# S5 mixer: state sums as TensorE matmuls, and the C array loaded once and copied on ScalarE

## The reference

```python
def s5_mixer(h, lam_re, lam_im, log_dt, b_re, b_im, c_re, c_im, d_skip, w_glu, b_glu):
    dt = jnp.exp(log_dt.astype(f32))[:, None]
    mag = jnp.exp(lr * dt)
    ab_re = mag * jnp.cos(li * dt)
    ab_im = mag * jnp.sin(li * dt)
    ...
    bu_re = jnp.einsum('blgp,gnp->blgn', u_c, bb_re)
    bu_im = jnp.einsum('blgp,gnp->blgn', u_c, bb_im)
    ...   # state s_t = ab * s_(t-1) + bu_t, complex, 64 groups x 64 states
    y = jnp.einsum('blgn,gpn->blgp', st_re, cr) - jnp.einsum('blgn,gpn->blgp', st_im, ci)
    ...
    y = (y + d_skip.astype(f32) * h.astype(f32)).astype(h.dtype)
    g = jax.nn.gelu(y)
    return g * jax.nn.sigmoid(g @ w_glu + b_glu)
```

## Time and profile before

| | us |
|---|---|
| median of three runs | 1295.19 |
| lowest and highest | 1292.33, 1297.12 |
| the profiled execution | 1296.42 |
| its span from first to last instruction | 1294.6 |

### The profile page before, as it was taken

The page is one execution under the profiler, slowest core; times in us unless marked ns, Lnnn a source line. Parts: engine busy times, 40 slices in busy tenths (PEclk is TensorE's granted clock), DMA queues, the critical chain, the costliest instruction groups (busy, mean ns, idle before and its releaser), DMA issues.

```text
span 1294.6 us, 25201 instructions
## 1 busy us (share of the span) xinstructions
PE 1247.5 (96%) x10872; PEld 1167.8 (90%) x10872; DVE 856.5 (66%) x1176; ACT 605.4 (47%) x778; POOL 51.8 (4%) x67
## 2 busy tenths in 40 slices
PE   5879999999999999999999999999999999999997
PEld 4667899999966489999999999999998999999997
DVE  6899678877547777768557565447469666666443
ACT  5854544433345465544345434336334545544342
POOL 5310000100000000000000000000000000000000
PEclk8968999999999999999999999999999999999998
DMA  9946568988742928654566554454454434655452
GB/s 261 311 152 204 200 227 287 333 290 270 223 156 93 298 93 280 208 194 155 166 199 195 163 179 162 155 177 155 145 167 149 146 131 131 196 194 188 146 179 73
DMA packets 219704, 247.01 MB, mean 191 GB/s; under 512 B 5872, under 2 KB 209088, under 8 KB 219616
## 3 DMA queue, kind: packets, MB, share of 16 engines
q1 hardware_dynamic: 211616, 218.63, 52.8%
q0 software_dynamic: 7648, 26.86, 6.1%
q10 hardware_dynamic: 352, 0.23, 0.1%
HBM read 244.66 MB, written 1.05 MB: 190 GB/s over the span
## 4 chain that ended last, share of the span: by engine, by line
PE 86%; DVE 5%; ACT 3%; DMA 3%; issue 1%; SPq 1%; DVEq 0%; ACTq 0%
PE PS L1749 85%; DMA RING<-in_ada_w 2%; SPq L441 1%; ACT PARTS L592 1%; DMA RING<-in_mla_w_uq 1%; DVE ARENA L1153 1%; DVE ARENA L1322 0%; DVE X L1157 0%; DMA RING<-in_w_in 0%; DVE ARENA L1350 0%; DVE PARTS L1011 0%; PE PS L2372 0%; DVE ARENA L1346 0%; DVE WL L1033 0%; PE PS L2088 0%
## 5 line engine op out<-in xcount | busy, mean ns | idle before, releaser
L1749 PE MATMUL PS<-PARTS 128*128 128x256 f32 (+3 forms) x3608 | 840.0, 283 | 0.0
L1749 PEld LDWEIGHTS PS<-PARTS 128*128 128x128 f32 (+1 forms) x3608 | 619.4, 189 | 1.4 <-issue 0.9
L1033 DVE TENSOR_TENSOR WL<-RING,PARTS 128x2048 fp32r<-128x2048 f32 (+2 forms) x189 | 387.3, 2053 | 241.1 <-ACT PARTS L592 240.6
L1749 PE MATMUL PS<-HH,WL 128*128 128x256 f32 (+3 forms) x1832 | 520.9, 284 | 2.0 <-DVE PARTS L1002 0.9
L1749 PE MATMUL PS<-HH,PARTS 128*128 128x256 f32 (+3 forms) x1832 | 518.6, 283 | 0.0
L592 ACT CAST PARTS<-RING 128x2048 fp32r<-128x2048 f32 (+2 forms) x189 | 324.1, 1717 | 306.5 <-DMA RING<-in_w_ffn_out 68.5
L1749 PEld LDWEIGHTS PS<-HH,WL 128*128 128x128 f32 (+1 forms) x1832 | 345.2, 188 | 7.9 <-issue 4.9
L1749 PEld LDWEIGHTS PS<-HH,PARTS 128*128 128x128 f32 (+1 forms) x1832 | 344.3, 188 | 0.4
L1749 PE MATMUL PS<-PARTS,WL 128*128 128x256 f32 (+1 forms) x832 | 236.9, 285 | 0.9 <-DVE PARTS L1648 0.5
L1749 PEld LDWEIGHTS PS<-PARTS,WL 128*128 128x128 f32 x832 | 158.2, 190 | 2.9 <-issue 2.1
L1749 PE MATMUL PS<-ARENA 128*32 128x63 f32 (+8 forms) x864 | 60.3, 279 | 2.8 <-DVE ARENA L1435 1.3
(11 more groups left out here) (349 smaller groups left out, 992.1 us busy)
## 6 DMA issues: line engine op xcount, KB each, us to landing
RING<-in_w_ffn_in SPq DMA_DIRECT2D x44, 1024.0 KB, 5.1
RING<-in_ada_w SPq DMA_DIRECT2D x32, 1024.0 KB, 8.7
RING<-in_ffn_w_gate SPq DMA_DIRECT2D x22, 1024.0 KB, 5.9
RING<-in_ffn_w_up SPq DMA_DIRECT2D x22, 1024.0 KB, 5.2
RING<-in_w_in SPq DMA_DIRECT2D x20, 1024.0 KB, 5.2
ARENA<-in_ada_w POOLq DMA_DIRECT2D x16, 1024.0 KB, 8.0
RING<-in_ffn_w_down SPq DMA_DIRECT2D x16, 768.0 KB, 4.8
RING<-in_w_ffn_out SPq DMA_DIRECT2D x16, 768.0 KB, 4.5
```

The lines of the kernel that those rows point to most:

```text
L1033: V.tensor_tensor(WL[:, u % SLOTS, 0:w], RING[:, u % SLOTS, 0:w], WH[:, u % SLOTS, 0:w].bitcast(fp32), SUB)\
L1749: return nc.tensor.matmul(o, lhsT, rhs, start=start, stop=stop)
```

## The change

Seven edits, all in the mixer:

1. **C loaded once.** GpSimd loads only the first half of `CRAW`, two DMAs in place of four. ScalarE waits for them and copies it into the second half (one copy of 128x1024), and counts `c_copies`; TensorE's transposes wait for that.
2. **Turn finished early.** VectorE's two operations that finish f (add of `RMUL`, clamp) move from behind `scaled(0)` to ahead of the waits before L1279. f and the whole part m exchange their arrays.
3. **Absolute value on VectorE.** |f| is now one `scalar_tensor_tensor` behind `scaled(0)`; ScalarE's Abs and its link go.
4. **Table load early.** ScalarE loads the table set of the sine before its second `row_copy`, where it had it just before the first sine.
5. **Tap 0 on TensorE.** `taps` is cut in two halves of four tiles. In each tile four matmuls of 32 rows by 32 columns add the diagonal through the identity; `k_out` copies all four taps, in eight copies of 32x512, and VectorE's four adds go. `y_of(0)` waits for the first half alone.
6. **State sums on TensorE for tiles 4 to 7.** `scan` ends with four multiplications of 128x256 (one pair with the sign in it); `states` goes. `y_of(4)` to `(7)` have 64 matmuls with 63 columns where they had 32.
7. **Order.** `ada_rows(7)` and `(8)` stand ahead of the taps, `ada_rows(9)` behind `y_of(2)`, ScalarE's `rows_copy` one tile later.

```diff
             for i, name in enumerate(("s5_c_re", "s5_c_im")):
-                for d in range(2):
-                    pool.dma_start(CRAW[:, i, :, d * NST:(d + 1) * NST],
-                                   A[name][0].rearrange("(k g) c n -> (g c) k n", g=8)).then_inc(S["cm_loaded"], 16)
+                pool.dma_start(CRAW[:, i, :, 0:NST], A[name][0].rearrange("(k g) c n -> (g c) k n", g=8)).then_inc(S["cm_loaded"], 16)
...
+            act.wait_ge(S["cm_loaded"], 32)
+            nc.scalar.copy(CRAW[:, :, :, NST:], CRAW[:, :, :, 0:NST]).then_inc(S["c_copies"], 1)
             c_compact()
...
-            nc.scalar.activation(by_pair(SIN), by_pair(COS), ACT.Sin, scale=2 * PI_IN)
-            link(nc.scalar.activation(by_pair(COS), by_pair(COS), ACT.Abs))
+            nc.scalar.activation(by_pair(SIN), by_pair(SIN), ACT.Sin, scale=2 * PI_IN)
             nc.scalar.activation(by_pair(COS), by_pair(COS), ACT.Sin, scale=-TWO_PI, bias=hpi).then_inc(S["turn_sin"], 1)
...
+                if kt >= FOLD:
+                    for a in range(2):
+                        V.scalar_tensor_tensor(PS2[kt][:, :, a, :], z[:, :, a, :], 1.0 - 2.0 * a, SIN[:, :, kt, :], MUL, MUL)
+                        ins = V.tensor_tensor(z[:, :, a, :], z[:, :, a, :], COS[:, :, kt, :], MUL)
+                    ins.then_inc(S["s_done"], 1)
+                    return
...
-                ins = V.tensor_tensor(KWD[rows, :, 0, rows], KWD[rows, :, 0, rows], KTAPS[rows, :, 0, :], ADD)
-            ins.then_inc(S["k_used"], 1)
...
+                        if i == 0:
+                            for q in range(4):
+                                rows = slice(32 * q, 32 * q + 32)
+                                mm(KTAPS[rows, kt, 0, :], ident[rows, rows], KWD[rows, kt, 0, rows], False, False)
...
-                pe.wait_ge(S["k_used"], 2)
+                pe.wait_ge(S["k_used"], 1 if kt == 0 else 2)
...
+                            ins = mm(y[rows, 1:, t], CT4[t][i][:, kt, rows], PC2[kt][:, q, i, 0:NCH - 1], False, last and kt < FOLD)
+                            if kt >= FOLD:
+                                ins = mm(y[rows, 1:, t], CT4[t][i][:, kt, rows], PS2[kt][:, q, 1 - i, 0:NCH - 1], False, last)
...
-            taps()
             ada_rows(7)
             ada_rows(8)
+            taps(0)
+            taps(4)
             for kt in range(KT):
                 y_of(kt)
-                if kt == 0:
+                if kt == 2:
                     ada_rows(9)
```

More of the change, by code:

```diff
@@ L409, in x_of @@
             return X[:, :, TALL - N_TOK[n]:TALL]
+        FOLD = 4
         HP_LAST = {1: 1, 5: 2}
@@ L731, in k_out @@
             def k_out():
-                act.wait_ge(S["k_ready"], 1)
                 act.wait_ge(S["kw_laid"], 2)
-                for q in range(4):
-                    rows = slice(32 * q, 32 * q + 32)
-                    ins = nc.scalar.copy(KWD[rows, :, 1:, rows], KTAPS[rows, :, 1:, :])
-                ins.then_inc(S["k_used"], 1)
+                for b in range(2):
+                    act.wait_ge(S["k_ready"], b + 1)
+                    for q in range(4):
+                        rows = slice(32 * q, 32 * q + 32)
+                        ins = nc.scalar.copy(KWD[rows, 4 * b:4 * b + 4, :, rows], KTAPS[rows, 4 * b:4 * b + 4, :, :])
+                    ins.then_inc(S["k_used"], 1)
             def gelu(kt):
@@ L751, in _ @@
             b_blocks(1)
+            nc.scalar.preload_act_table_set("trig_and_small")
             row_copy(1)
@@ L778, in _ @@
                     w_highs("glu", kt - 1)
-                if kt == 3:
+                if kt == 4:
                     rows_copy()
@@ L1275, in _ @@
             link(V.tensor_tensor(f, f, m, SUB))
+            link(V.tensor_tensor(f, f, RMUL[:, :, :], ADD))
+            link(V.tensor_scalar(f, f, 0.5, -0.5, ALU.min, ALU.max))
             dve.wait_ge(S["tr_ready"], 1)
@@ L1363, in _ @@
             turned_in(4)
-            dve.wait_ge(S["k_used"], 1)
-            for q in range(4):
-                rows = slice(32 * q, 32 * q + 32)
-                ins = V.tensor_tensor(KWD[rows, :, 0, rows], KWD[rows, :, 0, rows], KTAPS[rows, :, 0, :], ADD)
-            ins.then_inc(S["k_used"], 1)
             for kt in range(4, KT):
@@ L1373, in _ @@
                 scan(kt)
-                states(kt)
             w_lows("glu", 0)
@@ L2065, in _ @@
             ins.then_inc(S["meta_ready"], 1)
-            pe.wait_ge(S["cm_loaded"], 64)
+            pe.wait_ge(S["c_copies"], 1)
             pe.wait_ge(S["res_ready"], KT)
@@ L2082, in bt_of @@
                     if k == 0:
-                        pe.wait_ge(S["ct_used"], 1)
+                        pe.wait_ge(S["c_copies"], 2)
                     else:
@@ L2117, in b_u, with taps @@
                 ins.then_inc(S["bu_ready"], 1)
-            def taps():
+            def taps(kt0):
                 pe.wait_ge(S["bd_zero"], 1)
@@ L2124, in taps @@
                 pe.wait_ge(S["ct_exp"], CHUNK)
-                for kt in range(KT):
+                pe.wait_ge(S["kw_laid"], 1)
+                for kt in range(kt0, kt0 + 4):
                     for i in range(2):
@@ L2144, in y_of @@
                             rows = slice(32 * q, 32 * q + 32)
-                            ins = mm(y[rows, 1:, t], CT4[t][i][:, kt, rows], PC2[kt][:, q, i, 0:NCH - 1], False,
-                                     t == CHUNK - 1 and i == 1)
+                            last = t == CHUNK - 1 and i == 1
+                            ins = mm(y[rows, 1:, t], CT4[t][i][:, kt, rows], PC2[kt][:, q, i, 0:NCH - 1], False, last and kt < FOLD)
+                            if kt >= FOLD:
+                                ins = mm(y[rows, 1:, t], CT4[t][i][:, kt, rows], PS2[kt][:, q, 1 - i, 0:NCH - 1], False, last)
                 ins.then_inc(S["y_ready"], 1)
```

11 lines of the change are left out of this document (5 added, 6 removed).

## The result

Kernel before and changed kernel were run in turn, seven times each. The changed kernel takes 1302.46 us (median, 1300.75 to 1308.78), the kernel before 1293.40 us: a ratio of 1.0065, with a 95% interval of 1.0045 to 1.0084. It is slower, by some 8 us, where 3.8 us less had been forecast. The profiled executions lie closer together: 1300.75 and 1296.42 us, spans 1298.9 and 1294.6.

A forecast was written before the change was run, and what follows sets the result against it. TensorE was taken to bound the kernel, with time saved only where it waits or runs slowly in the mixer. -5.8 - 2.1 + 4.1 = -3.8 us, from 1295.19 to 1291.4; range 1286.5 to 1296.5.

The forecast's parts named there:

- 4.1 us more: `y_of` tiles 4 to 7: 32 added matmuls in each, 4 x 1.02 us, all on TensorE's path.
- without a wait of note: Kernel before, from 99.57 us on: TensorE goes through `y_of` and `glu`, which follow on each other's heels.
- -5.8: Start of `y_of(0)`: at 93.8 in place of 99.57, 5.8 us earlier.
- -2.1: At full clock `y_of(0)` takes 2.43 us, not 4.19, and `ada_rows(9)` 1.8, not 2.18: 2.1 us less.
- The 0.65 us at the modulation: VectorE's modulation at 51.47: gains between 0 and 0.65 us as the finish of f moves into idle time; 0.65 taken.
- Input products start at 64.1: VectorE's input products: 2.95 us earlier than 67.06, with the wait for ScalarE's second sine gone.
- `b_u` 4 to 7: TensorE's second half of `b_u`: after 3 to 4.5 us idle the clock falls, 13.9 us, from 69.2 to 83.1.
- Rival 1: Clock stays up through `b_u` 4 to 7, `y_of(0)` at 85.4, VectorE becomes the bound: -8.7, 1286.5 us; chance 0.12.
- `ada_rows` brings the clock back: Behind `b_u`, during `ada_rows(7)` and `(8)`: clock returns 4.6 us after the end of `b_u`, at 87.7.
- rival 2: Only the taps bring the clock back, not `ada_rows`; `y_of(0)` at 97.4: -0.2, 1295 us; chance 0.20.
- The slower rival: Added matmuls in `y_of` do not overlap; at 108 ns each they cost 13.8 us: +5.9, 1301 us; chance 0.08.
- I take the gain to last: Behind `y_of`: every wait hangs on TensorE, ScalarE or VectorE work that moves along, so the -3.8 us stays.

The follow-up runs named there:

- the two fastest kernels: Changed kernel with state sums on VectorE and `ada_rows(9)` behind `y_of(5)`: with SP holding ring unit 16 until `b_u(4)` is done, ratio 0.9971; without that hold, 0.9972.
- both groups of filling matmuls: 7 matmuls into an unused bank before `b_u(0)` and 12 before `b_u(4)`, added to the changed kernel with sums on VectorE, late `ada_rows(9)`, unit 16 held: ratio 0.9992.
- the last run: Changed kernel, sums of tiles 4 to 7 on TensorE, with `ada_rows(9)` late, ring unit 16 held and 7 plus 12 filling matmuls: ratio 1.0054.

## Why the prediction was wrong, step by step

- **The sum's missing term.** "4.1 us more" for the added matmuls was right as their own time: 2.04 us where 1.02 stood. The step that failed is that nothing else was charged to them. They also draw instructions: a tile of 144 records becomes one of 272, more than a block, and beside ring loads a block that takes less than some 6.5 us (up to 4.1 to the packet, 1.1 for it, 1.4 behind it) ends in a stop. In the whole kernel part 6 costs 7.5 us (0.58% on the kernel before) to 8.7 us (from 0.9998 to 1.0065). The 0.58 us of "issue" ahead of 115.89 in the earlier trace rows was the same thing, small, and was passed over ("without a wait of note"): a q8 packet ended at 114.42, 1.47 us ahead of 115.89.
- **The gain of the rest.** Part 6 is less than half of the miss: -3.8 us were forecast and some 8.4 more came, a miss of 12, of which the part beyond its 4.1 us is 3.4 to 4.6. The other terms, -5.8 and -2.1, make -7.9 us without the added matmuls, and the run with the sums back on VectorE measured 0.9998, -0.3 us (-3.2 to +2.6). In it `y_of(0)` came 2.9 us earlier and not 5.8, and with stops of 0.32 and 1.43 us and half clock behind the second `y_of` took 26.0 us, where 25.07 - 2.1 = 23.0 had been forecast. So it was again, beside slower taps, stops at block ends and half clock, for which nothing was charged; what was left at `glu`, 1.95 us, did not show in the time.
- **The front.** The 0.65 us at the modulation came (0.67). The next step, "Input products start at 64.1", failed: they waited 1.24 us for `b_u` and came at 65.66. The prediction moved the loads and VectorE, but not TensorE's idle time: TensorE was ready 2.3 us before `h` was, and ran `b_u` 0 to 3 at half clock. With C loaded twice they came at 63.93, `b_u` 4 to 7 took 69.04 to 82.97 at half clock and `y_of(0)` came at 93.82: the forecast's 64.1, 69.2 to 83.1 and 93.8, but in a kernel without part 1. That the last agrees is partly luck: the clock came back at 85.4 and not at 87.7, and the taps took 6.2 us and not 4.6.
- **`b_u` 4 to 7.** 69.2 to 83.1 were forecast and 71.41 to 84.7 came, but by another way: the idle time of 3 to 4.5 us before them was gone, since `b_u` 0 to 3 and `ada_rows` had ended late, the clock had come back at 70.4, and half of it ran at full clock, then came the stop, then half clock. That the end agrees is luck. Rival 1's clock was there for 4 us and was lost to the first stop.
- **`ada_rows` brings the clock back**: right (in full at 87.4, forecast 87.7); rival 2 is out. The taps took 89.49 to 95.74, 3.1 us a half where 2.3 were taken: a tap matmul at full clock costs 72 ns and was put at 54 (3.45 us for 64), and the small ones cost 50 ns each, not 37.
- **`y_of(0)`** came at 95.74, 1.9 us later than forecast, and at full clock, as forecast.
- **The slower rival** was the wrong mechanism: the weight loads overlap, at 32 ns for a matmul. Its 1301 is near what was measured, by luck, for a reason that no rival had.
- **"I take the gain to last"**: from `glu` to the norm 1.4 us more were lost, at a load of `in_ffn_w_gate` that took 9.90 us and had taken 8.5, and of 6.5 us there 2.2 had come back by the end of the span. These are two single executions; what decides it stays open.

Open are two things. In the two fastest kernels a stop of some 2.6 us remains ahead of `b_u(6)`. With both groups of filling matmuls it is absent (`b_u` 4 to 7 take 7.7 us without a stop), but the whole is not faster; how to be rid of it at a gain stays open. And the time from a block's start to its packet is not the ring loads' doing alone: at 84.4 us it was 3.1 us with no load under way, beside the slow matmuls of `ada_rows`; what TensorE must have done before it asks for a block was not shown.

## What to carry to other kernels

Price small matmuls on TensorE by their number too: 32 ns each is right only while some 256 instructions, weight loads included, last longer than the fetch of the next block, 3.4 us with the DMA idle and 5 to 6.7 us beside saturating loads in this kernel. Look for "issue" on TensorE's chain, count records between such stops, and move bulk loads away from the stretches with the most instructions per microsecond: here, with the sums on VectorE, moving one step is likely what turned no gain (0.9998) into one of 0.28% (0.9972). Work that is taken away ahead of TensorE can leave it idle and lower its clock, and so cost what it saves, as the single load of C did.

## What was not expected of the hardware

- TensorE's instruction blocks (some 256 records, 16.4 KB) arrive 3.4 to 6.7 us after the last one is begun, and both stops of over 2 us in the changed kernel were followed by half clock (for 10.2 and 6.8 us). It does not always follow: behind the one of 3.45 us in the last run the clock stayed at 1.00.
- The q8 packet comes late beside ring loads: 4.1 us after the block against 0.6 us without them for the same block. With each load cut in two it is 2.5 to 4.5 us, and the whole gains nothing.
- Idle times of 1.7 to 2.3 us before `b_u(0)` came with half clock over the next 13.7 to 17.1 us in seven kernels; in the kernel before, with part 6 alone and with C loaded twice, where `b_u(0)` follows at once, the clock stayed up. In the kernel with the late `ada_rows(9)`, sums on VectorE and no hold it was different again: 1.77 us idle, and the clock fell only at the end of a stop of 2.24 us in `b_u`.
